# Dilated attention in a one-core decoder trunk: value products with the values standing, two heads in the two halves of TensorE's columns, softmax weights divided before they are turned

## The reference, cut to what matters

```
out = einsum('bnrhqk,bnkrhe->bnqrhe', p / den, vw)
lse = (m + log(den))[..., 0]
...
wts = softmax(stack(lses), axis=0)
o = sum(wts[..., None] * stack(outs), axis=0)
y_b = o.reshape(bsz, s, DIL_OUT) @ b_w_out
```

## Time and profile before

| | |
|---|---|
| median of three executions | 1905.89 us |
| the profiled execution | 1905.4 us |
| its span | 1903.6 us |
| TensorE busy (matmul) | 1890.4 us, 99% |
| VectorE busy | 1540.5 us, 81% |
| ScalarE busy | 1225.4 us, 64% |
| mean granted TensorE clock | 0.997 |
| HBM, mean over the span | 273 GB/s |

### The profile page before, as it was taken

The page is one execution under the profiler, slowest core; times in us unless marked ns, Lnnn a source line. Parts: engine busy times, 40 slices in busy tenths (PEclk is TensorE's granted clock), DMA queues, the critical chain, the costliest instruction groups (busy, mean ns, idle before and its releaser), DMA issues.

```text
span 1903.6 us, 27279 instructions
## 1 busy us (share of the span) xinstructions
PE 1890.4 (99%) x10806; PEld 1655.3 (87%) x10806; DVE 1540.5 (81%) x1395; ACT 1225.4 (64%) x1095; POOL 70.6 (4%) x80
## 2 busy tenths in 40 slices
PE   9999999999999999999999999999999999999998
PEld 9989999999999988999988888888888888888886
DVE  8999865565568999764688888888888888888886
ACT  6555745454455565654577777777777777777775
POOL 1000000100010000000000000000000000000000
PEclk9999999999999999999999999999999999999999
DMA  9544544355545435553699999999999999999993
GB/s 338 182 159 145 188 162 181 133 189 183 192 165 187 166 133 197 179 184 127 244 363 384 378 384 363 406 373 379 374 359 401 378 374 385 352 412 373 375 397 113
DMA packets 76265, 521.39 MB, mean 274 GB/s; under 512 B 9360, under 2 KB 9616, under 8 KB 14992
## 3 DMA queue, kind: packets, MB, share of 16 engines
q1 hardware_dynamic: 72464, 507.84, 69.9%
q0 software_dynamic: 2992, 11.01, 2.0%
q10 hardware_dynamic: 720, 1.31, 0.2%
HBM read 512.79 MB, written 7.34 MB: 273 GB/s over the span
## 4 chain that ended last, share of the span: by engine, by line
PE 89%; DVE 5%; ACT 3%; issue 1%; DMA 0%; SPq 0%; ACTq 0%; DVEq 0%
PE psum L1671 21%; PE psum L1673 21%; PE psum L1672 21%; PE psum L1685 14%; PE psum L1686 7%; DVE wlo L1036 2%; ACT whi L564 2%; PE psum L2137 1%; PE psum L1893 1%; PE psum L1913 1%; PE psum L1832 1%; DVE U L1144 1%; DMA raw<-in_stream 0%; DVE U L1059 0%; PE psum L1810 0%
## 5 line engine op out<-in xcount | busy, mean ns | idle before, releaser
L1036 DVE TENSOR_TENSOR wlo<-raw,whi 128x2048 fp32r<-128x2048 f32 x477 | 1086.4, 2283 | 253.7 <-ACT whi L564 253.4
L564 ACT ACTIVATE whi<-raw 128x2048 fp32r<-128x2048 f32 x477 | 909.5, 1909 | 245.7 <-PE psum L1673 195.3
L1671 PE MATMUL psum<-whi,act_hl 128*128 128x512 f32 (+1 forms) x1472 | 567.5, 386 | 0.8
L1673 PE MATMUL psum<-whi,act_hl 128*128 128x512 f32 (+1 forms) x1472 | 560.2, 381 | 0.0
L1672 PE MATMUL psum<-wlo,act_hl 128*128 128x512 f32 (+1 forms) x1472 | 559.5, 380 | 0.0
L1685 PE MATMUL psum<-h_hl,whi 128*128 128x512 f32 x1216 | 431.5, 399 | 0.3 <-DVE U L1385 0.2
L1686 PE MATMUL psum<-h_hl,wlo 128*128 128x256 f32 x1216 | 340.4, 280 | 0.0
L1671 PEld LDWEIGHTS psum<-whi,act_hl 128*128 128x128 f32 x1472 | 276.9, 188 | 55.6 <-DVE wlo L1036 4.1
L1673 PEld LDWEIGHTS psum<-whi,act_hl 128*128 128x128 f32 x1472 | 276.8, 188 | 53.6
L1672 PEld LDWEIGHTS psum<-wlo,act_hl 128*128 128x128 f32 x1472 | 277.1, 188 | 51.4 <-issue 0.7
L1685 PEld LDWEIGHTS psum<-h_hl,whi 128*128 128x128 f32 x1216 | 228.4, 188 | 55.4 <-issue 0.7
(11 more groups left out here) (252 smaller groups left out, 1393.6 us busy)
## 6 DMA issues: line engine op xcount, KB each, us to landing
raw<-in_stream SPq DMA_DIRECT2D x474, 1024.0 KB, 6.7
raw<-in_stream SPq DMA_DIRECT2D x6, 512.0 KB, 3.7
U<-in_stream SPq DMA_DIRECT2D x2, 1024.0 KB, 11.8
xacc<-U POOLq DMA_DIRECT2D x3, 512.0 KB, 5.9
xT<-in_x_cols ACTq DMA_DIRECT2D x4, 256.0 KB, 6.7
raw<-in_stream SPq DMA_DIRECT2D x4, 256.0 KB, 7.5
memhat<-in_mem_cols SPq DMA_DIRECT2D x1, 1024.0 KB, 18.5
hrow<-U POOLq DMA_DIRECT2D x1, 1024.0 KB, 5.3
```

The costliest lines, as they stand in the source:

```text
L564: act.activation(whi[:, n % SPLIT, 0:words], src[:, 0:words], ACT.Copy).then_inc(hi_ready, 1)
L1036: dve.tensor_tensor(wlo[:, n % SPLIT, 0:words], src[:, 0:words], whi[:, n % SPLIT, 0:words].bitcast(F32), ALU.subtract).then_inc(lo_ready, 1)
L1671: pe.matmul(o, st[0], mv[0], start=start, stop=False, **kw)
L1673: return pe.matmul(o, st[1], mv[0], start=False, stop=stop, **kw)
```

## The change

The four `weigh` calls of a layer become two, each for two heads at once. The values (128 keys by 64) are now the standing operand and the transposed weights (128 keys by 128 queries) the moving one, so the output is 64 by 128 and comes out already turned. The two heads of a pair write partitions 0 to 63 and 64 to 127 of bank 4. The number of products is the same: 16 for a pair of heads. The pair (0, 1) stands before chunk 17, the pair (2, 3) before chunk 24, where `weigh(1)` and `weigh(3)` stood; before chunks 14 and 21 nothing stands any more. The four transposes before chunk 25 are gone.

As the queries now lie along the free dimension, the division by the sums moves ahead of the transposes. VectorE takes the reciprocal in `post(a+1)` (`head_den`), and ScalarE multiplies the weights by it in two instructions of 128x512 in `after_split(a+1)` (`head_norm`). `values(h)` waits for this. `head_out` is gone. The high and low parts of the output are made for each pair in `post(16)` and `post(23)`, in 128x256 pieces. `pT` has two buffers, one for each head of a pair; the second lies over part of `qT` and `kT`. `head_mask` waits in addition for the transposes of the head before.

```diff
             def head_exp(lay, h):
                 k = 4 * lay + h
                 act.wait_ge(mx_ready, k + 1)
-                if k:
-                    act.wait_ge(o_ready, k)
                 for b in range(TB):
                     ins = act.activation(prob[:, b, :], prob[:, b, :], ACT.Exp, bias=small[:, b:b + 1],
                                          accum_out=small[:, 4 + b:5 + b])
+                ins.then_inc(ex_ready, 1)
+
+            def head_norm(lay, h):
+                act.wait_ge(den_ready, 4 * lay + h + 1)
+                for b in range(TB):
+                    ins = act.activation(prob[:, b, :], prob[:, b, :], ACT.Copy, scale=small[:, 6 + b:7 + b])
                 ins.then_inc(pr_ready, 1)
...
-                if c == OT_AT:
-                    act.wait_ge(oT_done, lay + 1)
-                    act.activation(o_hi.rearrange("p a (l b) -> p a l b", b=TB),
-                                   bank[4][:].rearrange("p (a b l) -> p a l b", a=2, b=TB), ACT.Copy).then_inc(o_hi_s, 1)
+                for p in range(2):
+                    if c == HEAD_AT[2 * p + 1] + 3:
+                        act.wait_ge(pv_done, 2 * lay + p + 1)
+                        act.activation(o_hi[:, p, :].rearrange("p (l b) -> p l b", b=TB),
+                                       bank[4][:, 0:S].rearrange("p (b l) -> p l b", b=TB), ACT.Copy).then_inc(o_hi_s, 1)
...
                     if c == HEAD_AT[h]:
                         head_exp(lay, h)
+                    if c == HEAD_AT[h] + 1:
+                        head_norm(lay, h)
...
-            def head_out(lay, h):
+            def head_den(lay, h):
                 k = 4 * lay + h
-                dve.wait_ge(pv_done, k + 1)
-                mine(dve.reciprocal(small[:, 6:8], small[:, 4:6]))
-                settled()
-                for b in range(TB):
-                    ins = dve.tensor_scalar(otok[:, b, DH * h:DH * h + DH], head_bank(h, 0)[:, DH * b:DH * b + DH],
-                                            small[:, 6 + b:7 + b], None, ALU.mult)
-                ins.then_inc(o_ready, 1)
+                dve.wait_ge(ex_ready, k + 1)
+                dve.reciprocal(small[:, 6:8], small[:, 4:6]).then_inc(den_ready, 1)
...
                 dve.wait_ge(sc_done, k + 1)
+                if k:
+                    dve.wait_ge(pt_done, k)
...
-                for h in range(HEADS):
-                    if c == HEAD_AT[h] + 3:
-                        head_out(lay, h)
+                for p in range(2):
+                    if c == HEAD_AT[2 * p + 1] + 3:
+                        dve.wait_ge(o_hi_s, 2 * lay + p + 1)
+                        dve.tensor_tensor(o_lo[:, p, :].rearrange("p (l b) -> p l b", b=TB),
+                                          bank[4][:, 0:S].rearrange("p (b l) -> p l b", b=TB),
+                                          o_hi[:, p, :].bitcast(F32).rearrange("p (l b) -> p l b", b=TB),
+                                          ALU.subtract).then_inc(o_lo_s, 1)
...
                 if c in CONV_A_AT and c not in HEAD_AT:
                     conv_a_ops(lay, CONV_A_AT[c])
+                for h in range(HEADS):
+                    if c == HEAD_AT[h] + 1:
+                        head_den(lay, h)
...
                 else:
-                    pe.wait_ge(o_ready, 4 * lay + 2)
+                    pe.wait_ge(o_lo_s, 2 * lay + 1)
...
-            def weigh(lay, h):
-                k = 4 * lay + h
-                pe.wait_ge(pT_ready, k + 1)
-                if h == 0:
+
+            def weigh(lay, p):
+                pe.wait_ge(pT_ready, 4 * lay + 2 * p + 2)
+                if p == 0:
                     s_, val = taken(BASE[lay] + AT["v", 2])
                     pe.wait_ge(s_, val)
                 for b in range(TB):
                     for j, (g, t) in enumerate(KEY_BLOCKS[b]):
-                        at = 256 * g + DH * h
-                        ins = pe.matmul(head_bank(h, 0)[:, DH * b:DH * b + DH], pT[:, b, P * j:P * j + P],
-                                        vtok[:, t, at:at + DH], start=j == 0, stop=j == 3)
+                        for h in range(2):
+                            at = 256 * g + DH * (2 * p + h)
+                            ins = pe.matmul(bank[4][64 * h:64 * h + 64, P * b:P * b + P], vtok[:, t, at:at + DH],
+                                            pT[h][:, 2 * b + j // 2, P * (j % 2):P * (j % 2) + P], start=j == 0, stop=j == 3)
                 ins.then_inc(pv_done, 1)
...
-                    if c == OT_AT + 1:
-                        pe.wait_ge(o_ready, 4 * lay + 4)
-                        for i in range(2):
-                            for t in range(TB):
-                                ins = pe.transpose(bank[4][:, 256 * i + P * t:256 * i + P * t + P],
-                                                   otok[:, t, P * i:P * i + P], ident[:])
-                        ins.then_inc(oT_done, 1)
```

More of the change, by code:

```diff
@@ L53 @@
 KEY_BLOCKS = (((0, 0), (0, 1), (1, 0), (2, 0)), ((1, 1), (2, 1), (0, 0), (0, 1)))
-OT_AT = 24
 CONV_C_AT = {16: (0, 1), 19: (2, 3)}
@@ L140, in trunk @@
         gates = u(6776, DB, S)
-        prob, pT = u(9856, 2, 512), u(10880, 2, 512)
-        otok = u(12160, TB, HEADS * DH)
+        prob, pT = u(9856, 2, 512), (u(10880, 4, 256), u(0, 4, 512)[:, :, 0:256])
         merged = u(12672, DB, S)
@@ L242, in trunk @@
         a_f, a_hi_s, a_lo_s = sem("a_f"), sem("a_hi_s"), sem("a_lo_s")
-        sc_done, mx_ready, pr_ready, pt_done, pT_ready, pv_done, o_ready = (
-            sem(s_) for s_ in ("sc_done", "mx_ready", "pr_ready", "pt_done", "pT_ready", "pv_done", "o_ready"))
-        oT_done, o_hi_s, o_lo_s = sem("oT_done"), sem("o_hi_s"), sem("o_lo_s")
+        sc_done, mx_ready, ex_ready, den_ready, pr_ready, pt_done, pT_ready, pv_done = (
+            sem(s_) for s_ in ("sc_done", "mx_ready", "ex_ready", "den_ready", "pr_ready", "pt_done", "pT_ready", "pv_done"))
+        o_hi_s, o_lo_s = sem("o_hi_s"), sem("o_lo_s")
         mg_hi_s, mg_lo_s = sem("mg_hi_s"), sem("mg_lo_s")
@@ L640, in head_pT @@
                 for b in range(TB):
-                    ins = act.activation(pT[:, b, :], head_bank(h, b), ACT.Copy)
+                    ins = act.activation(pT[h % 2][:, 2 * b:2 * b + 2, :], head_bank(h, b).rearrange("p (a b) -> p a b", a=2),
+                                         ACT.Copy)
                 ins.then_inc(pT_ready, 1)
@@ L1306, in post @@
                                              -float(D) / AW, aacc, op0=ALU.mult, op1=ALU.add).then_inc(ln_xc, 1)
[L1307 to L1312, removed]
                 if c == MEM_AT[0]:
@@ L1868, in _ @@
                             values(lay, h)
-                        if c == HEAD_AT[h] + 4:
-                            weigh(lay, h)
+                    for p in range(2):
+                        if c == HEAD_AT[2 * p + 1] + 4:
+                            weigh(lay, p)
                     for p in range(2):
@@ L1940, in _ @@
                     elif what == "bout":
-                        pe.wait_ge(o_lo_s, lay + 1)
+                        pe.wait_ge(o_lo_s, 2 * lay + 2)
                         chunk_out(n, o_hi, o_lo, 2, mean_sum if c == LN_AT[0] + 1 else None)
```

## The result

The changed kernel takes 1920.4 us (median of 4, 1920.01 to 1921.6) against 1905.96 for the kernel before (median of 4); the ratio is 1.0075, 95% interval 1.006 to 1.0089. It is slower, by 14.4 us where 11 were forecast. The profiled execution took 1920.14 us, its span is 1918.4.

A forecast was written before the change was run, and what follows sets the result against it. TensorE was taken as the bound, 89% of the chain. Profiled 1905.4 us plus 10.0 for waits less work saved, 1.4 for the clock and 0.5 for the median gave 1917 us, range 1910 to 1921.5.

The forecast's parts named there:

- What TensorE gains: Two weigh calls and four transposes fewer a layer, pair calls 2.0 us each: 3.4 us less work a layer, 6.8 in all.
- What is added ahead of the transposes: Reciprocal 0.16 us and two multiplications 1.35: transposes can start 1.59 us after VectorE would go on to its next split.
- The stands: TensorE's waits before the heads' transposes: about 17 us together over both layers, the two longest near 5.4 us.
- Head 3: First layer, before head 3's transposes: head_norm stands behind ScalarE's split, table load and sigmoid; TensorE stands 5.4 us, shift +6.00.
- What I cost at nothing: Waits for output parts in post(16) and post(23), and splits behind them, cost 0; about 2 us if cover went.
- TensorE's clock: Clock may fall in the two head-3 stands: 0 to 5.6 us, taken as 1.4 us for one fall.
- Halves in turn: Rival: column halves run one after the other, each pair 3.4 us instead of 2.0: +5.6, 1923 us; chance 0.10.
- Faster, divided weights in time: Rival: head_norm of head 3 ends before TensorE arrives, the stands go, 6.8 us less work remain: 1899 us; chance 0.05.
- one that falls away: TensorE's 0.16 us wait before chunk 23 on VectorE's low part of the short convolution goes: -0.41 us, first layer.
- the waits less the work saved: Both layers: waits of about 17 us against 6.8 us of work saved, 5.45 + 4.56 = 10.0 us slower.

The follow-up runs named there:

- e2: Changed kernel with weigh's loop over the two heads outermost, so eight products of one head run in a row, then eight of the other: 1926.38 us.
- e9: The order of e8 with the old products (eight weigh calls, four transposes before chunk 25, head_out multiplying by 1.0): 1905.83 us, ratio 0.9999 to the kernel before.
- e8: Changed kernel with all divisions early as in e7, plus the short convolution's gate product and its high and low parts earlier: 1897.73 us, ratio 0.9957.
- e3: Changed kernel with only head 3's reciprocal and multiplications moved early, into post(21) on VectorE and ScalarE: 1910.06 us, ratio 1.0016 to the kernel before.
- e6: Changed kernel with head 3's multiplications ahead of table load and sigmoid, still behind chunk 24's split, reciprocal unmoved: 1914.31 us.
- e1: Changed kernel with 20 fp32 identity products put on TensorE before head 3's transposes, to keep it busy in the stand: 1917.4 us.
- e7: Changed kernel with all heads' reciprocals and the multiplications of heads 1 to 3 moved early into post(a+1): 1901.33 us, ratio 0.9976 to the kernel before.
- e5: Kernel before with only the division moved ahead of the transposes, products in their old form, head_out multiplying by 1.0: 1920.21 us, ratio 1.0078.
- e4: Changed kernel without the softmax's division (no head_den, head_norm or their waits): 1902.77 us, ratio 0.998 to the kernel before.

## Why the prediction was right

- **What TensorE gains: right.** The pair's call was put at 2.0 us. It takes 1.97 with its tail, 1.90 to the next chunk, and e2 shows why. The saving of 6.8 us in all is what e9 against e8 measures: 6.6 in spans, 8.1 in medians. The Trainium skill's rule that outputs in different column groups run at once (TensorE: Matmul & The Clock Gate, section on packing small matmuls) agrees; the 0.2 us over 1.70 stays as a cost of entry and exit.
- **What is added ahead of the transposes: right.** The multiplications take 1.32 to 1.34 us where 1.35 was taken from the tail's L1006. The stands were worked out as 0.88, 1.98, 1.02 and 5.4 us, and the trace has 0.72, 1.82, 0.85 and 5.20, each short by 0.2: TensorE's idle time is counted from its last matmul's modelled end. In the second layer, against head 0, heads 1 to 3 start 0.07, 1.35 and 4.98 us later than before; forecast 0.19, 1.51 and 5.12.
- **Head 3: right, with a second bound behind it.** What ends last in the trace is ScalarE, as forecast, and e3 shows that the place is the cause, together with the reciprocal's. The table load and the sigmoid alone are some 2 us of 5.2 (e6). Behind ScalarE's place the reciprocal's would still hold TensorE for 2.6 us, by the estimate under e3, which the prediction doesn't weigh.
- **What I cost at nothing: right.** No row has TensorE waiting for the parts of the output, or for the splits behind them.
- **TensorE's clock: the mechanism right, the size too small.** I took one fall, at 1.4 us. It fell at both stands. TensorE worked at half pace from 161.62 to 166.88 and from 716.16 to 719.84, 8.9 us, half of which is 4.5 (the 8.2 us and 4.1 that e1's expectation has were read too short); e1 gives 4.0 over the same work. This term is short by 2.6, most of the difference between 11 and 14.4. The bound of 0 to 5.6 held it. I made the price smaller because I could not say whether it would fall; the one row I had, 2.9 us of idleness against stands of 5.4, spoke more for both than for one.
- **Rivals.** Halves in turn is excluded by the trace and by e2. "Faster, divided weights in time" is what e7 built: I gave 1899 us, and e7 took 1901.33, as the low part of the short convolution then bound chunk 23. With that wait removed, e8 goes to 1897.73. I had listed that wait as one that falls away and not asked when it comes back. The condition I named for this rival, the multiplications ahead of the sigmoid, was not enough: e6 meets it and takes 1914.31.

The sum, between the spans of the profiled executions, is 14.8 us. 4.0 are the clock in the two stands. Another 1.5 stand far behind them, where the change touches nothing. In the second layer's feed-forward part TensorE is 13.2 us behind the kernel before at one set of transposes and 14.7 at the next; first the kernel before, then the changed one:

```profile
950.63 0.60 PE L2137 MATMUL psum<-ident,U 128*128 128x128 f32 x4
...
971.07 0.60 PE L2137 MATMUL psum<-ident,U 128*128 128x128 f32 x4
```

```profile
963.83 0.60 PE L2137 MATMUL psum<-ident,U 128*128 128x128 f32 x4
964.26 3.64 PE L2072 MATMUL psum<-U 128*128 128x10 f32 x32
...
985.81 0.60 PE L2137 MATMUL psum<-ident,U 128*128 128x128 f32 x4
```

Between them the changed kernel's trace has the clock at half, with TensorE busy throughout, and the kernel before has not:

```profile
968.00:969.00 1.00, 1.00 (x6) 0.78 (x6) 1.00 (x1) 0.00 (x0) 0.00 (x0) 1.00 0.92 360
969.00:970.00 1.00, 1.00 (x4) 0.81 (x3) 0.23 (x1) 0.00 (x0) 0.00 (x0) 0.50 1.04 442
...
972.00:973.00 1.00, 1.00 (x5) 0.82 (x4) 0.00 (x0) 0.74 (x1) 0.00 (x0) 0.79 0.99 418
```

That leaves 9.3 us for the waits less the work saved, where I had worked out 10.0. So the prediction missed 2.6 us of the clock in the stands and all of the 1.5 behind them, and had 0.7 too much in the waits. The 1.5 is chance and no part of the argument: such a fall stands in the traces of the change, e3, e5, e6 and e7, and in none of the kernel before, e1, e4, e8 and e9; in e2 it lasts 6.8 us.

## What to carry to other kernels

Before moving an operation ahead of the engine that bounds the kernel, find its place in the other engine's order, and read what stands in front of it there, on every engine that it needs; here the place of two multiplications of 0.7 us and one reciprocal of 0.15 cost 10.3 us over two layers (e3), more than three times their length. Work saved on a bound engine is real only where its next operand is already there, so a saving should be tried together with the order that feeds it. And count a stand of the matrix engine of some microseconds with the half-speed stretch that can follow.

## What the runs showed of the hardware

The granted clock did not follow the length of TensorE's stand. It fell 3.6 us and 2.0 us after the stop in the change, 1.3 us after work had begun again in e6 (at 161.02, back at 164.42, 3.4 us at half), and not at all after 3.03 us in e6's second layer. In the change each stretch at half clock was 6.8 us long, in e5, with stands of 3.7 us, 3.4. What sets the moment stays open; a stand of 3 us may or may not pay.

It fell without a stand too: in the change at 969.0 us, back at 972.4, with TensorE busy in every slice. What TensorE had done before were 32 matmuls of 10 moving columns, 964.26 to 967.75. The kernel before does the same 32 at 951.07, and its clock stays at 1.00 up to 965. That fall cost 1.5 us, so a difference of this size between two kernels of this series can be the clock alone.

Two fp32 products in the two halves of the columns overlap as those in the halves of the partitions do: 32 matmuls of 128 moving columns in 1.90 us alternating, 3.26 us in turn.
